# Retention of a two-layer hybrid block on one core: half-array matmul pairs, compact queries, and squares moved behind the weight splits

## The reference, cut to what matters

```
def step(state, inp):                      # one chunk of 128 positions, all heads
    qi, ki, vi = inp
    scores = einsum('bhnd,bhmd->bhnm', qi, ki) * inner_decay
    out = einsum('bhnm,bhme->bhne', scores, vi) \
        + einsum('bhnd,bhde->bhne', qi, state) * q_decay[..., None]
    state = state * chunk_decay + einsum('bhmd,bhme->bhde', ki * k_decay[..., None], vi)
    return state, out
...
o_r = rms_norm(o_r, ret_norm_g) ; o_r = o_r * silu(gate_r) ; y_r = o_r @ ret_w_o
```

## Time and profile before

| | |
|---|---|
| median of 3 runs | 975.29 us (975.02 to 976.36) |
| the profiled execution, its own time | 975.27 us |
| its span, first to last instruction | 973.5 us |
| PE busy | 947.0 us, 97% of the span |
| DVE, ACT, POOL busy | 43%, 42%, 49% |
| mean granted clock of PE | 0.998 of full |
| block `retention(KD)`, from PE's first scores to group 5's first matmul | 133.30 to 157.69 us |

### The profile page before, as it was taken

The page is one execution under the profiler, slowest core; times in us unless marked ns, Lnnn a source line. Parts: engine busy times, 40 slices in busy tenths (PEclk is TensorE's granted clock), DMA queues, the critical chain, the costliest instruction groups (busy, mean ns, idle before and its releaser), DMA issues.

```text
span 973.5 us, 13086 instructions
## 1 busy us (share of the span) xinstructions
PE 947.0 (97%) x4792; PEld 769.2 (79%) x4792; DVE 422.8 (43%) x998; ACT 405.5 (42%) x892; POOL 472.9 (49%) x448
## 2 busy tenths in 40 slices
PE   6999999999999999999999999999999999999998
PEld 5778788887888877777767888789888877778777
DVE  3200138144114433657475514416666584465531
ACT  5333342334224353445455332226535364455531
POOL 3443445534546644564343443544467838534342
PEclk9999999999999999999999999999999999999999
DMA  6333211322333332222221243322324321100013
GB/s 220 108 88 87 71 60 44 91 83 87 108 88 107 87 87 65 66 66 65 66 65 44 75 145 106 104 91 83 87 81 126 109 85 45 45 22 1 23 44 108
DMA packets 41167, 78.71 MB, mean 81 GB/s; under 512 B 3296, under 2 KB 5088, under 8 KB 41104
## 3 DMA queue, kind: packets, MB, share of 16 engines
q1 hardware_dynamic: 40240, 76.30, 26.2%
q10 hardware_dynamic: 864, 1.57, 0.6%
HBM read 75.74 MB, written 2.12 MB: 80 GB/s over the span
## 4 chain that ended last, share of the span: by engine, by line
PE 84%; DVE 6%; POOL 3%; ACT 3%; issue 2%; DMA 1%; SPq 1%; ACTq 0%; DVEq 0%; POOLq 0%
PE Z L1586 23%; PE Z L1588 21%; PE Z L1587 21%; PE A L1811 4%; PE A L1819 2%; PE A L1713 1%; PE A L1726 1%; PE A L1596 1%; PE A L1586 1%; PE A L1779 1%; POOL w_lo L815 1%; PE A L1588 1%; PE A L1587 1%; PE Z L1670 1%; DMA raw<-in_w_in 1%
## 5 line engine op out<-in xcount | busy, mean ns | idle before, releaser
L815 POOL TENSOR_TENSOR w_lo<-raw,w_hi 128x512 fp32r<-128x512 f32 (+1 forms) x262 | 341.9, 1313 | 407.5 <-ACT w_hi L522 407.0
L1586 PE MATMUL Z<-w_hi,hT_hi 128*128 128x512 f32 (+1 forms) x832 | 337.7, 406 | 3.3 <-DVE hT_lo L1049 1.2
L1588 PE MATMUL Z<-w_hi,hT_lo 128*128 128x512 f32 (+1 forms) x832 | 323.9, 389 | 0.0
L1587 PE MATMUL Z<-w_lo,hT_hi 128*128 128x512 f32 (+1 forms) x832 | 323.3, 389 | 0.0
L522 ACT CAST w_hi<-raw 128x512 fp32r<-128x512 f32 (+1 forms) x262 | 157.5, 615 | 265.5 <-PE Z L1588 242.9
L1586 PEld LDWEIGHTS Z<-w_hi,hT_hi 128*128 128x128 f32 x832 | 156.4, 188 | 44.4 <-issue 8.7
L1588 PEld LDWEIGHTS Z<-w_hi,hT_lo 128*128 128x128 f32 x832 | 156.2, 188 | 32.8
L1587 PEld LDWEIGHTS Z<-w_lo,hT_hi 128*128 128x128 f32 x832 | 156.7, 188 | 26.7
L639 ACT ACTIVATE x_sb<-x_sb,nmax 128x128 f32<-128x128 f32 (+3 forms) x64 | 35.5, 557 | 40.0 <-DVE nmax L1275 40.0
L1586 PE MATMUL Z<-w_hi,oT_hi 128*128 128x512 f32 x128 | 51.1, 399 | 0.5 <-DVE pT L1110 0.5
L1588 PE MATMUL Z<-w_hi,oT_lo 128*128 128x512 f32 x128 | 50.0, 391 | 0.0
(11 more groups left out here) (220 smaller groups left out, 1379.7 us busy)
## 6 DMA issues: line engine op xcount, KB each, us to landing
raw<-in_w_in SPq DMA_DIRECT2D x92, 512.0 KB, 3.8
raw<-in_w_out SPq DMA_DIRECT2D x16, 512.0 KB, 3.7
raw<-in_ret_w_o SPq DMA_DIRECT2D x8, 512.0 KB, 3.3
raw<-in_diff_w_o SPq DMA_DIRECT2D x8, 512.0 KB, 3.4
x_sb<-in_x SPq DMA_DIRECT2D x8, 256.0 KB, 4.9
x_sb<-in_x SPq DMA_DIRECT2D x4, 512.0 KB, 4.4
out<-x_sb SPq DMA_DIRECT2D x8, 256.0 KB, 3.2
raw<-in_w_in SPq DMA_DIRECT2D x4, 416.0 KB, 3.2
```

Source lines behind the costliest of these rows:

```text
L815: pool.tensor_tensor(w_lo[:, s % SPLIT_SLOTS, 0:width], raw[:, c % RAW_SLOTS, s - CHUNK_START[c], 0:width], w_hi[:, s % SPLIT_SLOTS, 0:wid ...
L1586: pe.matmul(out, l_hi, r_hi, start=first, stop=False)
L1587: pe.matmul(out, l_hi, r_lo, start=False, stop=False)
L1588: return pe.matmul(out, l_lo, r_hi, start=False, stop=last)
```

## The change

Queries are stored once, on all 128 partitions (`ret_queries` is now 128 by 512), and ACT copies them in one instruction. `scores` and the cross term are done head by head with 64-deep matmuls of 128 columns: head 0 on rows 0 to 63 of the array, head 1 on rows 64 to 127, one after the other in the code. `updates` becomes matmuls of 64 output rows: head 0 to partitions 0 to 63 of A3, head 1 to 64 to 127. The three chunks now fit A3, and A2 holds nothing but transposes, so the wait for the turned queries in `updates` and one in `turn_pair` go. `states` reads whole partitions, 3 instructions instead of 6. A0 now holds one head's scores and A1 the other's, and PE waits once for both decays where it waited twice for halves. The zeroing of the query tiles (4 instructions of DVE early in the kernel) goes. The squares go on POOL between the splits of groups 5 and 6, and DVE's sums behind all four pairs.

```diff
@@ act: turned_q
-                    for hh in range(2):
-                        rows = slice(RDK * hh, RDK * (hh + 1))
-                        last = act.copy(ret_queries(p)[rows, hh, :], A[2][rows, :])
-                    last.then_inc(r_turned, 1)
+                    act.copy(ret_queries(p), A[2][:, :]).then_inc(r_turned, 1)
@@ pool
+            def ret_square(h):
+                pool.wait_ge(r_o, h + 1)
+                square(o_sb[:, :, RDV * h:RDV * (h + 1)], 512)
...
                     lo(SLAB0[g] + k)
+                    if g == G_RET + 2:
+                        ret_square(5 + k)
...
                     lo(SLAB0[g] + k)
+                    if g == G_RET + 1:
+                        ret_square(k - 3)
@@ dve: states
+                    link(dve.tensor_copy(st[:, 0, :], A[3][:, 0:P]))
+                    for c in (1, 2):
+                        last = dve.scalar_tensor_tensor(st[:, c, :], st[:, c - 1, :], chunk_c[:, p:p + 1],
+                                                        A[3][:, P * c:P * (c + 1)], ALU.mult, ALU.add)
...
-                    if p > 1:
-                        head_sums(p - 2)
-                head_sums(pairs - 1)
+                for p in range(pairs):
+                    head_sums(p)
@@ pe: turn_pair
-                    if job >= 3:
-                        pe.wait_ge(r_sf, job // 2)
@@ pe: scores
-                    for i in range(2):
-                        if p:
-                            pe.wait_ge(r_pf, 2 * p - 1 + i)
-                        for c in (2 * i, 2 * i + 1):
-                            cc = slice(P * c, P * (c + 1))
-                            last = pe.matmul(A[i][:, 256 * (c % 2):256 * (c % 2 + 1)], rk[:, p % 2, cc], q[:, :, cc],
-                                             start=True, stop=True)
-                        last.then_inc(r_s, 1)
+                    if p:
+                        pe.wait_ge(r_pf, 2 * p)
+                    for c in range(TT):
+                        cc = slice(P * c, P * (c + 1))
+                        for hh in range(2):
+                            rows = slice(RDK * hh, RDK * (hh + 1))
+                            last = pe.matmul(A[hh][:, cc], rk[rows, p % 2, cc], q[rows, cc], start=True, stop=True)
+                            if c == TT - 1:
+                                last.then_inc(r_s, 1)
@@ pe: updates
-                        if c == 2:
-                            pe.wait_ge(r_turned, max(2 * p + 2, 3))
-                        out = (A[3], A[3], A[2])[c][:, 256 * (c % 2):256 * (c % 2 + 1)]
-                        last = pe.matmul(out, kd_f[:, p % 2, c, :], v[:, c, :], start=True, stop=True)
+                        for hh in range(2):
+                            rows = slice(RDK * hh, RDK * (hh + 1))
+                            last = pe.matmul(A[3][rows, P * c:P * (c + 1)], kd_f[:, p % 2, c, rows],
+                                             v[:, c, P * hh:P * (hh + 1)], start=True, stop=True)
@@ pe: cross term
-                    for hh in range(2):
-                        if po:
-                            pe.wait_ge(r_o, 2 * po - 1 + hh)
-                        for c in range(1, TT):
-                            cc = slice(P * c, P * (c + 1))
-                            last = pe.matmul(Z[2 + hh][:, cc], q[:, hh, cc], st_f[:, po % 2, c - 1, :], start=True, stop=True)
-                        last.then_inc(r_x, 1)
+                    if po:
+                        pe.wait_ge(r_o, 2 * po)
+                    for c in range(1, TT):
+                        cc = slice(P * c, P * (c + 1))
+                        for hh in range(2):
+                            rows = slice(RDK * hh, RDK * (hh + 1))
+                            last = pe.matmul(Z[2 + hh][:, cc], q[rows, cc], st_f[rows, po % 2, c - 1, :],
+                                             start=True, stop=True)
+                            if c == TT - 1:
+                                last.then_inc(r_x, 1)
```

More of the change, by code:

```diff
@@ L214, in build @@
         with ExitStack() as scope:
-            ret_f = sb("ret_f", [P, 2, 2, 2, 2, P], F32, scope)
+            ret_f = sb("ret_f", [P, 2, 2, TT, P], F32, scope)
             rq1 = sb("rq1", [P, 2, S], F32, scope)
@@ L391, in ret_queries @@
         def ret_queries(p):
-            return rq1 if p % 2 else rq0
+            return (rq1 if p % 2 else rq0)[:, 0, :]
         def ret_values(p):
@@ L599, in retention @@
                 if stage == 1:
-                    act.wait_ge(q_zeros, 2)
                     turned_q(0)
@@ L1197, in states @@
                     st = st_f[:, p % 2, :, :]
[L1198 to L1212, removed]
+                    link(dve.tensor_copy(st[:, 0, :], A[3][:, 0:P]))
+                    for c in (1, 2):
+                        last = dve.scalar_tensor_tensor(st[:, c, :], st[:, c - 1, :], chunk_c[:, p:p + 1],
+                                                        A[3][:, P * c:P * (c + 1)], ALU.mult, ALU.add)
+                        if c == 1:
+                            link(last)
                     last.then_inc(r_sf, 1)
@@ L1224, in retention @@
                     if p < pairs:
-                        for i in range(2):
-                            if p > 1:
[L1227 to L1231, removed]
+                        if p > 1:
+                            dve.wait_ge(r_i, 2 * p - 2)
+                        for hh in range(2):
+                            dve.wait_ge(r_s, 2 * p + hh + 1)
+                            dve.tensor_tensor(ret_f[:, p % 2, hh, :, :], A[hh][:, :].rearrange("p (c n) -> p c n", c=TT),
+                                              decay[:, 2 * p + hh, :].unsqueeze(1).broadcast_to([P, TT, P]),
                                               ALU.mult).then_inc(r_pf, 1)
@@ L1545, in _ @@
                     dve.engine_nop().then_inc(lam_dots, 1)
[L1546 to L1553, removed]
                     dve.wait_ge(row_mm, 1)
@@ L1665, in retention @@
                         pe.wait_ge(r_xe, 2 * po)
+                    pe.wait_ge(r_pf, 2 * po + 2)
                     for c in range(TT):
-                        if c % 2 == 0:
-                            pe.wait_ge(r_pf, 2 * po + c // 2 + 1)
                         for hh in range(2):
-                            last = pe.matmul(Z[hh][:, P * c:P * (c + 1)], ret_f[:, po % 2, c // 2, c % 2, hh, :],
+                            last = pe.matmul(Z[hh][:, P * c:P * (c + 1)], ret_f[:, po % 2, hh, c, :],
                                              v[:, c, P * hh:P * (hh + 1)], start=True, stop=True)
```

5 lines of the change are left out of this document (removed).

## The result

The changed kernel takes **969.23 us** (median of 3 runs, 969.1 to 969.67) where 975.29 was measured before: a ratio of 0.9937, 95% interval [0.9923, 0.995]. It is faster by 6.06 us; forecast were 969.9 us and a range from 967.8 to 973.4.

The account below looks back on a forecast made before the run. The prediction took PE's own time to bound the kernel (26.43 of 28.00 us busy). Terms 6.6 + 1.3 + 1.3 - 3.4 - 0.4 = 5.4 us took 975.3 to 969.9 us, range 967.8 to 973.4.

Parts of the forecast that it names:

- The bursts: Scores, cross terms and updates: halves work side by side, n records take n/2 + 1 slots; 6.6 us less.
- if starts keep their order: In half-array bursts: float32 records start as queued, two per half, so n records need n/2 + 1 slots of 0.11 us.
- The switches: PE changing between whole array and halves, in the block and group 4: 20 switches at 0.17 us, 3.4 us lost.
- The wait for A2: Updates of pairs 2 and 3: third chunk no longer waits for A2, 0.67 us each, 1.3 us less.
- The copy of the queries: Groups 3 and 4: ACT's single copy shortens PE's wait for POOL's split, 0.65 us twice, 1.3 us less.
- What is late next: Block's end: new wait of about 0.2 us before the last inner product, DVE's first sum 0.2 later; 0.4 us lost.
- The squares: POOL, groups 5 and 6: square and split take 2.33 us within a 2.72 us slab, and PE has three slabs' lead.
- The sum: Whole kernel: 6.6 + 1.3 + 1.3 - 3.4 - 0.4 = 5.4 us less, from 975.3 to 969.9 us.
- The first: Rival: column halves of the updates do not overlap, 2.0 us of the gain gone, 971.9 us; chance 0.15.
- the second: Rival: weight loads of the updates' column halves are exposed, a burst takes 2.6 us, 977.3 us; chance 0.03.
- The third: Rival: no pair of half-array float32 matmuls overlaps while switches stay, 976.5 us, slower; chance 0.10.
- The fourth: Rival: freed time partly waited away at hand-overs between transposes, ACT's copies and PE, or slower splits; 972 to 973 us; chance 0.12.

Follow-up runs that it names:

- The heads issued apart: Changed kernel with the loops of scores, cross terms and updates turned round, all of head 0 before head 1; 972.64 us.
- More switches: Changed kernel with the cross terms of pairs 0 and 1 cut into three pieces between the inner product's chunks, 8 more mode changes; 971.19 us.
- fewer switches: Changed kernel with last pair in A0 to A3, plus bursts reordered for 2 switches less per pair in pairs 0 and 1; 966.7 us.

## Why the prediction was right

**The bursts** were the step that was mis-sized, by 1.2 us. A burst of n records takes n/2 slots and not n/2 + 1: 0.89 us for scores, 0.67 for the cross term, 0.66 for the updates (the first four records of the changed scores start at 131.966, 131.973, 132.180 and 132.186 us). The step "if starts keep their order" failed: the halves go record by record although a float32 matmul is two records. The heads issued apart show that this can be: there, records of one half start ahead of queued ones of the other. By the same count as in the prediction, 4 x 0.83 + 3 x 0.67 + 4 x 0.63 = 7.85 us in place of 6.6.

**The switches** were right: 3.5 us in place of 3.4. Measured by how far the end of a burst's first record stands behind the end before it (0.30 us, for example, where records follow each other by 0.11), going into row halves costs 0.19 us, into column halves 0.14, from columns to rows 0.19, out to a whole matmul of the inner product or the projections 0.195, and out to the transposes 0.15. More switches and fewer switches gave the same price from two sides.

**The wait for A2** went, 1.3 us, as summed. But the prediction gave it to the third chunk's new place; with the updates whole it stays away too, so the short copy would have sufficed for it. **The copy of the queries** brought 1.45 us in groups 3 and 4 in place of 1.3: around the two matmuls that waited for a split, from the start of the matmul ahead to the start of the matmul behind, it takes 0.77 and 0.68 us less (99.56 - 98.27 = 1.29 us before, 99.94 - 99.42 = 0.52 after, for the first). In the block it was worth another 1.05 us, which the sum held without a line of its own: with two copies the gain of the A2 term would have gone to the scores' wait.

**What is late next** was right: a new wait of 0.34 us (0.2 forecast), and from the last inner product to group 5 4.19 us where there were 4.14 (0.2 forecast). Together 0.4, as forecast. The squares cost PE nothing between the splits, as argued, and their move brought 0.17 us in the profiled executions.

**The sum** by measured terms: 7.85 + 1.34 + 1.45 - 3.5 - 0.4 = 6.7 us, and the two distances give 6.77. The medians differ by 6.06, and by 7.3 in the repetition (976.0 to 968.69); between them lies start-up, which no term here touches. So it is partly luck that the forecast of 5.4 us stands within 0.7 of the first result: it is 1.3 us short of what the terms brought and 1.9 short of the repetition, nearly all of the former in the bursts.

**The rivals.** The first and the second fell by the updates' burst of 0.81 us for 12 records. The loads of column halves overlap here: those 12 records, each with a weight load of its own, take six slots. The Trainium skill says in "TensorE: Matmul & The Clock Gate", section The mechanism, that loads overlap running matmuls only when the row group differs; this trace disagrees. The third, that no pair overlaps, was the right thing to fear: without overlap in scores and cross term alone the kernel stands at 976.67 us, of which eight gaps of 0.32 us between the halves, less the waits that they hide, are the experiment's own. The fourth did not come; the margin of the copies is thin, though: two copies cost 2.5 us, and with the cross term split up ACT's copy of the keys was 0.27 us late.

## What to carry to other kernels

A matmul that uses half of the array's rows or of its output columns is worth issuing in pairs, the two halves alternating in the code: here two then cost what one costs (16 records in 8 slots of 0.11 us), in float32. Price the changes of mode by themselves, 0.14 to 0.2 us each, and put bursts of one mode next to each other: pairing eight records saves 0.44 us, and one switch in and one out cost 0.38. An instruction taken from an engine that PE does not wait for by name can still be worth more than its own time, if a cast and a split stand behind it.

## What the runs showed of the hardware that was not expected

PE starts records of the other half ahead of records that were queued before them (head 1's first at 133.200 us, head 0's last at 133.529), so that even two heads issued one after the other take 12 slots for their scores, halfway between the 8 of full pairing and the 16 of none.

The same program can lose or keep 0.7 us in a later place. From group 5 to the end most runs took 815.7 to 815.9 us, but two took 815.0 and 815.1. The difference lies in the second layer's attention, which no edit touched. In the changed kernel (timeline of PE):

```profile
786.03 0.33 PE L1802 MATMUL A<-ident,prob 128*128 128x128 f32 x1 [0.93 <-POOL prob L940]
787.56 0.36 PE L1568 MATMUL A<-kT_hi,qT_hi 128*128 128x256 f32 x1 [1.21 <-DVE q_lo L1326]
...
788.57 0.68 PE L1568 MATMUL Z<-hT_hi,w_hi 128*128 128x512 f32 x1
...
793.00 0.39 PE L1568 MATMUL A<-kT_hi,qT_hi 128*128 128x512 f32 x1
```

Busy times and granted clock there:

```profile
788.00:789.00 1.00, 1.00 (x9) 0.95 (x8) 1.00 (x7) 0.93 (x4) 0.14 (x1) 0.84 0.21 64
789.00:790.00 1.00, 1.00 (x4) 0.76 (x3) 1.00 (x2) 1.00 (x3) 1.00 (x1) 0.50 0.00 0
```

After two waits of 0.93 and 1.21 us the granted clock falls to 0.50 (1.2 GHz) for some 3 us. In the kernel with fewer switches the same rows, with the same two waits, run at full clock (the last line has busy times and granted clock, columns as above):

```profile
782.41 0.33 PE L1805 MATMUL A<-ident,prob 128*128 128x128 f32 x1 [0.94 <-POOL prob L940]
783.94 0.36 PE L1568 MATMUL A<-kT_hi,qT_hi 128*128 128x256 f32 x1 [1.19 <-DVE q_lo L1326]
...
784.94 0.48 PE L1568 MATMUL Z<-hT_hi,w_hi 128*128 128x512 f32 x1
...
788.69 0.47 PE L1568 MATMUL A<-kT_hi,qT_hi 128*128 128x512 f32 x1 [0.70 <-DVE kT_lo L1331]
...
785.00:786.00 1.00, 1.00 (x7) 0.87 (x6) 1.00 (x4) 0.94 (x3) 0.76 (x1) 1.00 0.01 4
```

The same work takes 793.00 - 788.57 = 4.43 us in one and 788.69 - 784.94 = 3.75 in the other, where 0.70 of it is already a wait for DVE. Nine of the eleven traces show this fall, and the two without it, no overlap and fewer switches, are the two that took 815.0 and 815.1. It is not the program that decides: in the repetition of the changed kernel the two executions with a mean granted clock of 1.000 took 968.14 and 968.59 us, the three with 0.998 took 968.69 to 969.03. Why the clock falls in one execution and not in another stays open; it is part of the spread that start-up does not explain.
